# A hybrid decoder layer: the decode stream beside the prompt's input projection and attention

## What is computed

```python
def mixer_inputs(x, mod, w_in, cos, sin):
    z = modulate(x, mod[:, 0], mod[:, 1]) @ w_in            # 1024 -> 3072 columns
    h, gb, gc, q, k, v = jnp.split(z, SPLIT_IDX, axis=-1)   # 512 columns each
    q, k = apply_rope(q...), apply_rope(k...)
    return h, gb, gc, q, k, v

# prompt: causal differential attention over its own 1024 tokens, 4 heads, 2 components
y_conv = gb * short_conv(gc * h, conv_w)
s = q . k * QK_HEAD ** -0.5;  p = softmax(s);  a = p[:, :, 0] - lam * p[:, :, 1];  o = a @ v
# sample: the same, with k and v = gathered pages of cache_k, cache_v, then the new tokens
k_past = cache_k[l, page_table];  v_past = cache_v[l, page_table]
# both: output projection, adaLN gate, layer norm, SwiGLU of width 2816, gate, layer norm
```

## Time and profile before

| | us |
|---|---|
| median of 3 runs | 2172.3 (2167.52 to 2173.88) |
| the profiled execution, its own time | 2174.06 |
| span of its profile | 2172.3 |
| adaLN modulation | 0 to 97 |
| prompt turned and split | 97 to 120 |
| input projection, by feature | 122 to 262 |
| input projection, by token | 265 to 411 |
| sample's q, k, v; barrier; page numbers | 411 to 432 |
| decode stream, keys alone | 432 to 509 |
| decode stream beside the prompt's attention | 509 to 1056 |
| decode stream, values alone | 1056 to 1139 |
| output projection to the end | 1139 to 2172 |

### The profile page before, as it was taken

How to read it: one execution, slowest core, us unless ns; L and a number is a source line. 1 busy time by engine, 2 the same in 40 slices (tenths; PEclk the granted TensorE clock), 3 DMA queues, 4 the chain that set the end, 5 groups by cost and what they waited for, 6 DMA issues and landing times.

```text
span 2172.3 us, 39883 instructions
## 1 busy us (share of the span) xinstructions
PE 1791.4 (82%) x17492; PEld 1460.1 (67%) x17492; DVE 1049.0 (48%) x1596; ACT 542.2 (25%) x1151; POOL 321.1 (15%) x287
## 2 busy tenths in 40 slices
PE   4789999756777877777656957999999998999991
PEld 1267899644555555565546956777777776999991
DVE  2234221288788788888405573111112111566567
ACT  0210111003334234244212031112111110444441
POOL 0000000033333333333221026000000000000003
PEclk8799999858998889889857988999999999999996
DMA  9801123299999999999974100121121122611112
GB/s 301 310 20 40 57 78 116 81 406 397 411 387 408 413 408 404 406 392 415 340 272 175 58 20 20 59 96 58 58 77 58 58 64 88 226 45 45 45 35 99
DMA packets 133275, 404.29 MB, mean 186 GB/s; under 512 B 12153, under 2 KB 76665, under 8 KB 100338
## 3 DMA queue, kind: packets, MB, share of 16 engines
q0 software_dynamic: 37392, 270.55, 30.9%
q1 hardware_dynamic: 93666, 130.67, 17.8%
q10 hardware_dynamic: 2080, 1.05, 0.2%
HBM read 377.79 MB, written 24.51 MB: 185 GB/s over the span
## 4 chain that ended last, share of the span: by engine, by line
PE 65%; DMA 16%; DVE 14%; issue 3%; ACT 2%; POOL 0%; SPq 0%; DVEq 0%; ACTq 0%; POOLq 0%
PE psum L764 29%; PE psum L1051 12%; PE psum L772 11%; DMA v_ring<-cache_v,page_idx 10%; DVE k_ring L1489 4%; DMA ada_w<-w_ada 3%; PE psum L896 2%; PE psum L833 2%; PE psum L853 2%; PE psum L747 2%; DMA k_ring<-cache_k,page_idx 2%; DVE soft L1432 1%; DVE x_lo L1330 1%; PE psum L710 1%; DVE p_t L441 1%
## 5 line engine op out<-in xcount | busy, mean ns | idle before, releaser
L1489 DVE STREAM_TRANSPOSE k_ring<-k_ring 128x2048 f32<-128x2048 f32 x128 | 294.5, 2303 | 9.8 <-DMA k_ring<-cache_k,page_idx 9.5
L764 PE MATMUL psum<-x_hi,w_hi 128*128 128x512 f32 x896 | 281.3, 395 | 0.0
L764 PE MATMUL psum<-x_lo,w_hi 128*128 128x512 f32 x896 | 277.2, 391 | 0.0
L764 PE MATMUL psum<-x_hi,w_lo 128*128 128x512 f32 x896 | 275.9, 389 | 0.0
L1349 DVE TENSOR_TENSOR w_lo<-w_raw,w_hi 128x2048 fp32r<-128x2048 f32 x37 | 86.9, 2350 | 362.5 <-ACT w_hi L1109 352.6
L896 PE MATMUL psum<-v_ring,p_t 128*32 128x128 f32 x4096 | 161.3, 305 | 75.3 <-DMA v_ring<-cache_v,page_idx 73.5
L1051 PE MATMUL psum<-d_hi,h_hi 128*128 128x256 f32 x704 | 202.8, 288 | 13.1 <-DVE d_lo L1743 11.2
L1051 PE MATMUL psum<-d_lo,h_hi 128*128 128x256 f32 x704 | 200.2, 284 | 0.0
L1051 PE MATMUL psum<-d_hi,h_lo 128*128 128x256 f32 x704 | 200.0, 284 | 0.0
L764 PEld LDWEIGHTS psum<-x_hi,w_hi 128*128 128x128 f32 x896 | 165.6, 188 | 44.8 <-ACT h_out L1242 4.5
L764 PEld LDWEIGHTS psum<-x_lo,w_hi 128*128 128x128 f32 x896 | 168.7, 188 | 35.7
(11 more groups left out here) (228 smaller groups left out, 2610.5 us busy)
## 6 DMA issues: line engine op xcount, KB each, us to landing
ada_w<-w_ada SPq DMA_DIRECT2D x12, 2048.0 KB, 9.9
w_raw<-w_in SPq DMA_DIRECT2D x12, 1024.0 KB, 5.3
w_raw<-w_gate SPq DMA_DIRECT2D x11, 1024.0 KB, 5.4
w_raw<-w_up SPq DMA_DIRECT2D x11, 1024.0 KB, 6.2
h_store<-h_out SPq DMA_DIRECT2D x11, 1024.0 KB, 7.7
h_all<-h_store SPq DMA_DIRECT2D x11, 1024.0 KB, 8.9
d_raw<-w_down SPq DMA_DIRECT2D x44, 256.0 KB, 2.9
x_rows<-x_prompt SPq DMA_DIRECT2D x2, 2048.0 KB, 17.4
```

The costliest lines, as they stand in the source:

```text
L764: last = mm(psum[:, 2 * ft + c, 0:CH], w[:, s, k, ft * P:(ft + 1) * P], x[:, k, c * CH:(c + 1) * CH], start=k == 0 and j == 0, stop=k == K ...
L1489: v.transpose(group, group).then_inc(k_turned, 1)
```

## The change

Stages 2 and 3 become one. The sample tokens no longer share the prompt's weight blocks: their whole projection runs first, in 6 blocks of 512 columns loaded for them alone (`w_sample`, 2 MB each), one after each of the first 6 steps of the prompt's projection. So `w_in` is read twice. POOL's gathers start when these 6 products are done.

There are now 180 **turns** (`TURNS`), and `upto` gives the slots that lie in each:

- turns 0 to 23, half a **unit** of 128 convolution columns each (`half_unit`, 24 products of 512 tokens); a unit's weights are half a MB in pieces of 512 bytes, two buffers. Slots 0 to 21 lie in turns 10 to 23 (`FIRST`), 1 or 2 in a turn, keys alone.
- turns 24 to 71, one token tile of a 256-column block each (`tile_in`), 8 turns a block, blocks in the order q, k, v, q, k, v. Slots 22 to 69: two in the first turn of a block, none in the fifth, one in each other. `block_raw`, `block_hi`, `block_lo` and `z_rows` have one buffer each. Three PSUM banks (5 to 7) take the results of units and tiles, where there were four pairs.
- turns 72 and 73, two slots each. SP stores the last block, waits for it, and fetches head 0's keys and queries and all values of the prompt.
- turns 74 to 179, the prompt's attention as before, with 81 slots spread over 106 turns.

`k_ring` has 4 buffers instead of 5. The gates of the adaLN (`gate_p`, `gate_s`) give their room to the convolution: they are written to DRAM after stage 1 and fetched again ahead of `x1`, and `xs_rows` is fetched again too. What comes after the merged stage is as before.

```diff
-    GP, RK, RV = 4, 5, 3
+    GP, RK, RV = 4, 4, 3
+        FIRST = 10
+        upto = [0] * FIRST + [round((LAG - 2) * (p + 1 - FIRST) / (HALVES - FIRST)) for p in range(FIRST, HALVES)]
+        for p in range(TILES_IN):
+            upto.append(upto[-1] + {0: 2, 4: 0}.get(p % NT, 1))
+        upto += [upto[-1] + 2, upto[-1] + 4]
+        rest = SLOTS - upto[-1]
+        upto += [upto[-1] + rest * (p + 1) // (TURNS - HEAD0) for p in range(TURNS - HEAD0)]
...
-            pool.wait_ge(stage_done, 8)
-            pool.wait_ge(conv_s_in, 96)
-            pool.dma_start(v_rows[:], v_out.rearrange("(t p) n -> p t n", p=P)).then_inc(v_in_rows, 16)
+            pool.wait_ge(s_done, 2 * BLOCKS)
             pool.wait_ge(page_idx_ready, GP)
             load_pages(pool)
...
+            def keep_tile(n):
+                j, t = n // NT, n % NT
+                act.wait_ge(tm_done, n + 1)
+                if n == 0:
+                    act.wait_ge(y_conv_kept, 16 * (CC // P))
+                    act.wait_ge(conv_stored, 16 * (CC // P))
+                elif t == 0:
+                    act.wait_ge(z_stored, 16 * j)
+                copy(z_rows[:, t, :], psum[:, DENSE + n % 3, 0:WB]).then_inc(tm_free, 1)
...
+                for n in slots_at(p):
+                    slot(n)
+                if p < HALVES:
+                    half_unit(p)
+                    if p < BLOCKS:
+                        sample_in(p)
+                    if 1 <= p <= BLOCKS:
+                        fold_sample_in(p - 1)
+                    if p == BLOCKS + 2:
+                        turn_queries()
+                elif p < HALVES + TILES_IN:
+                    tile_in(p - HALVES)
...
             sp.wait_ge(o_turned, NT)
+            sp.dma_start(gate_p[:], gate_store[0:1].rearrange("o g d -> (o g) d").partition_broadcast(P)).then_inc(gates_in, 16)
+            sp.dma_start(gate_s[:], gate_store[1:1 + QUAD]).then_inc(gates_in, 16)
             sp.dma_start(x1[:], x_dram.rearrange("(t p) d -> p t d", p=P)).then_inc(x1_in, 16)
```

More of the change, by code:

```diff
@@ L531, in _ @@
-            for n in range(2, NB_IN):
-                load_w(n, w_in, in_cols[n])
-                if n == 6:
-                    sp.wait_ge(conv_ready, 1)
-                    with nc.allow_non_contiguous_dma(reason="two tokens' rows by feature"):
-                        for f in range(CC // P):
-                            sp.dma_start(io["new_conv_prompt"][0, 0][:, f * P:(f + 1) * P].rearrange("j p -> p j"),
-                                         u_conv[:, f, T:T + 2]).then_inc(conv_stored, 16)
-                if n - 2 >= 6:
-                    store_z(n - 8)
@@ new lines, in store_conv, with store_y @@
+            def store_conv(f):
+                sp.wait_ge(conv_ready, f + 1)
+                with nc.allow_non_contiguous_dma(reason="two tokens' rows by feature"):
+                    sp.dma_start(io["new_conv_prompt"][0, 0][:, f * P:(f + 1) * P].rearrange("j p -> p j"),
+                                 u_conv[:, T:T + 2]).then_inc(conv_stored, 16)
+            def store_y(f):
+                sp.wait_ge(fm_free, 6 * f + 6)
+                sp.dma_start(y_conv_store[f * P:(f + 1) * P, :], y_conv_f[:]).then_inc(y_conv_kept, 16)
@@ new lines, in store_z @@
+            def store_z(j):
+                half, which = j // 3, j % 3
+                if which < 2:
+                    sp.wait_ge(roped, 2 * half + which + 1)
+                else:
+                    sp.wait_ge(tm_free, TB + NT * (j + 1))
+                to = (q_store, k_out, v_out)[which]
+                sp.dma_start(to[:, half * WB:(half + 1) * WB].rearrange("(t p) n -> p t n", p=P), z_rows[:]).then_inc(z_stored, 16)
+            for p in range(HALVES):
+                if p % 2 == 0 and 2 + p // 2 < UNITS_IN:
+                    load_unit(2 + p // 2)
+                if p < BLOCKS - 2:
+                    load_sample(p + 2)
+                if p == 9:
+                    store_sample()
+                if p % 6 == 5:
+                    store_conv(p // 6)
+                if p > 6 and p % 6 == 1:
+                    store_y(p // 6 - 1)
@@ L555, in _ @@
             sp.wait_ge(conv_stored, 16 * (CC // P))
[L556 to L566 removed]
+            sp.wait_ge(y_conv_kept, 16 * (CC // P))
@@ new lines, in tile_in @@
+            def tile_in(n):
+                j, t = n // NT, n % NT
+                pe.wait_ge(w_lo_done, UNITS_IN + j + 1)
+                if n < 3:
+                    pe.wait_ge(fm_free, HALVES - 2 + n)
+                else:
+                    pe.wait_ge(tm_free, TB + n - 2)
+                at = slice(t * P, (t + 1) * P)
+                for k in range(KC):
+                    w_low = block_lo[k // (KC // 2)][:, k % (KC // 2), :]
+                    for i, (w, x) in enumerate(((block_hi[:, k, :], x_hi), (block_hi[:, k, :], x_lo), (w_low, x_hi))):
+                        last = mm(psum[:, DENSE + n % 3, 0:WB], x[:, k, at], w,
+                                  start=k == 0 and i == 0, stop=k == KC - 1 and i == 2)
+                last.then_inc(tm_done, 1)
@@ new lines, in sample_in @@
+            def sample_in(n):
+                if n == 0:
+                    pe.wait_ge(xs_ready, 1)
+                    pe.wait_ge(x_banks_free, 4 + UNITS)
+                pe.wait_ge(ada_in[n % 2], 16 * (z.MODS + n // 2 + 1))
+                pe.wait_ge(s_quads_free, 2 * n)
+                for k in range(KC):
+                    q = QUAD * (k % 4)
+                    last = mm(psum[q:q + QUAD, n % 2, :], x_t_in[:, k, :], w_sample[:, n % 2, k, :],
+                              start=k < 4, stop=k >= KC - 4)
+                last.then_inc(s_done, 2)
@@ new lines, in fold_sample_in, with turn_queries @@
+            def fold_sample_in(n):
+                pe.wait_ge(s_quads_free, 2 * n + 4)
+                if n >= 2:
+                    pe.wait_ge(s_fold_free, 2 * n)
+                mm(psum[0:QUAD, 2 + n % 2, :], C("quad_fold"), quads_in[:, n % 2, :], start=True, stop=True).then_inc(s_folded, 2)
+            def turn_queries():
+                pe.wait_ge(q_wide_ready, 1)
+                for hb in range(4 * H):
+                    last = mm(psum[:, 4, hb * BS:(hb + 1) * BS], q_wide[:, hb].rearrange("p a j -> p (a j)"),
+                              ident[0:QUAD, 0:QUAD], start=True, stop=True)
+                last.then_inc(q_all_done, 1)
@@ L955, in slot @@
                     by_query(b - 2)
-            for n in range(SLOTS):
-                h, u, q = dense_at(n)
+            for p in range(TURNS):
+                h, u, q = dense_at(p)
                 if u is None and q == 1:
@@ L1426, in maxima @@
+            ROPED = [j for j in range(BLOCKS) if j % 3 < 2]
             def maxima(u, c):
```

510 lines of the change are left out of this document (302 added, 208 removed).

## The result

The changed kernel takes 2178.1 us in the median (20 runs, 2171.2 to 2189.1) against 2169.4 for the kernel before (20 runs, 2159.8 to 2183.0). The ratio is 1.0045, 95% interval 1.003 to 1.006: slower by 0.45%. I had forecast 2160, so the sign was wrong; the time lies in the range.

The account below looks back on a forecast made before the run. PE was taken to bound the projection and full DMA engines the attention, whose turns were almost as slow by themselves. The merged stage's terms ended at 1124 against 1139; with 3 us after it, -12, so 2160 us, range 2100 to 2230.

Parts of the forecast that it names:

- so 547 - 41 - 45 = 461: Prompt's attention, turns 75 to 179: 547 us minus 41 of value waits and 45 of work moved or gone gives 461.
- the 22 for fifty transposes: Attention: fifty fewer key transposes, a third of them holding up a tile's chain by 1.3 us, save 22 us.
- rival B: Attention: the tile's chain, not its slots, sets 506 us; blocks wait 8 us; 2211 us in all; chance 0.20.
- The 15 for softmax moved ahead: Attention: a quarter of the sample's softmax pieces on DVE and ACT moved ahead, estimated to save 15 us.
- Turns 0 to 23: Units, sample projection and first key groups: 187 us from a start at 119, so turn 24 starts at 306.
- Turns 24 to 71: Projection tiles beside the stream: PE 262, block starts 21, waits for stores 32, sum 315 us; turn 72 at 621.
- The store term: Projection tiles: each block waits 0 to 9 us for the previous block's store, taken as 6.5 x 5 = 32.
- handoffs "at an estimated 0.15": Projection: handoffs between PE's pieces at 0.15 us each; 96 of them beside the tiles, 14 us.
- Turns 72 to 75: Before head 0's keys: last store, k and q queue behind about 11 outstanding gathers, 41 us, bounds 20 and 67.
- After it: After the merged stage: refetched gates delay x1 by 0 to 3 us; with xs_rows, 3 us taken.
- Rival A: Merged stage: transfers set the pace, stores land within PE's 19 us, head 0's fetches take 25; 2109 us; chance 0.20.
- Rival C: Projection tiles: coupled engine lists stall, a turn costs 8 us instead of 6.6, 384 instead of 315; 2229 us; chance 0.10.

## Why the prediction was wrong

**What bounds the attention.** I had read that "taking slots out of these turns helps only where a slot was on the tile's chain", and that most of the worth depends on this. That was the right question with the wrong answer in figures. The runs by the groups in the attention:

| run | groups | attention, us | waits for values | PE idle | clock |
|---|---|---|---|---|---|
| stream where it was, new code | 207 | 555 | 35 | 135 | 0.88 |
| no slots in the units' turns | 176 | 530 | 28 | 141 | 0.86 |
| the changed kernel | 132 | 489 | 0 | 147 | 0.85 |
| PE's groups alone | 132 | 433 | - | 120 | 0.87 |
| no stream | 0 | 488 | - | 242 | 0.57 |

(Groups are the records of the two lines divided by 32, PE idle is length less busy time.) From 207 to 132 groups the attention gains 66 us, but 35 of that are waits for values; the other 75 groups' work gives 31 (some us less if the 555 is too long, as said above), or 0.4 us a group, where PE alone takes 0.98 for one.

**The term that failed** is "so 547 - 41 - 45 = 461": 489 was measured, 28 more. The waits for values did go (43.0 us in the whole of 508 to 1055), and the 22 for fifty transposes is made likely by the 15 to 24 us that fifty others were worth. What I left out is that a value wait or a slot also covers the tile's chain. While PE waited for a value group, maximum, exponentials and combining went on; take the wait away and PE arrives earlier at the same chain. I counted these covers as pure gain. The chain waits grew by 62 us (34.8 + 26.5 for `a_rows` and `e_rows`, 0.5 for `a_t`). In the account of PE the attention became 58 us shorter: 77 us less busy, 43 us less waiting for values, and 62 us more waiting for the chain. Two runs bear it out: with nothing of the stream but PE's groups these waits are 115 of after's 125 us, and with 22 slots put back they fall to 92. A smaller part is the clock: it fell from 0.88 to 0.85, and the attention's own products grew from 184 to 193 us by their lines, of which some 2 us are records missing from the trace before. This is rival B, to which I gave 0.20, by the mark that I had set for it ("if PE's waits for `a_rows`, `a_t` and `e_rows` grow by 40 us or more, B"), at about six tenths of its price: it said 506, and the attention came out above the 473 that I had named as the point from which the change is slower.

The 15 for softmax moved ahead was an estimate whose share of the listed rows is not worked out, and the 8 for the last 35 turns has no row behind it; no run here measures them apart.

**Turns 0 to 23** ended as forecast: last unit product near 306, first key group at 199.5. Turn 24's two slots began at 305.9 for 306 forecast, but its first tile began at 317. In the run without a stream PE waited 10 us for block 0's lower halves there (277.6 to 287.6), and I had charged 2 (within the next stretch). In the changed kernel the lower halves were ready at 311.9. PE stood for 7.4 us in the second slot, before a transpose of the softmax, until DVE had copied the one before it to `p_t` (314.90 to 316.12), and this copy stood behind the lower halves and a key transpose in DVE's list. Error +9.

**Turns 24 to 71**: 315 forecast, 299 measured. The store term was 32, and the run with half stores shows 34. The rest I put at 283; counted from turn 24's slots, as the forecast did, it was 276 there (308.0 to 583.7). The handoffs "at an estimated 0.15" are the likeliest to have been too high: between the stalls a turn with one slot takes 4.95 us (602.64 to 607.59), where 2.9 + 2 x 0.98 + 2 x 0.15 gives 5.16, or 10 us more in 48 turns.

```profile
600.45 1.01 PE psum L989 x32
601.46 0.87 PE psum L1008 x32
602.33 0.31 PE psum L1021 x2
602.64 3.07 PE psum L889 x24
...
607.59 3.07 PE psum L889 x24
```

The store did not cost 6.5 us in each block but 10 to 11 us in every second one (PE stood before 385.9, 486.7 and 590.6), 32.7 in all: the total of 32 was met, by luck, with each stall mis-sized. **Turns 72 to 75**: 41 forecast, 34 measured; the reason given, the outstanding gathers, is shown by the fetches' 4.6 and 5.9 us once they are held back, and by the 10.5 us without a stream. **After it**: +3 forecast, +4.5 measured (the stage ends where it ended before, the span is 4.5 longer), with a fetch of `x` of 16.3 us in the chain. In the sum:

| | forecast | measured | difference |
|---|---|---|---|
| start, and turns 0 to 23 | 306 | 317 | +11 |
| turns 24 to 71 | 315 | 299 | -16 |
| turns 72 to 75 | 41 | 34 | -7 |
| attention | 461 | 489 | +28 |

That is +16, which leads from 1123 to 1139 and from a saving of 12 us to a loss of 4.5 in the profiled executions (8.7 in the medians). The first two rows are cut at the first tile; cut at turn 24's slots, as in the forecast, they are 0 and -5. Misses of -12 ahead of the attention covered nearly half of its +28: that is luck.

**Rival A** asked for stores that land in under 12 us; the quickest took 16.6, and four took over 26. With them the Trainium skill's figure ("DMA: Bandwidth & Descriptors", Specifications), that pieces from 512 bytes on reach line rate, does not carry over to a store that shares the engines: this one has pieces of 1 KB and moved at 1.05 MB / 26.4 us = 40 GB/s. **Rival C** fell as well: a turn of turns 24 to 71 cost 299 / 48 = 6.2 us, not 8.

**Where the expected gain went.** PE's idle time is where it was: 36 us of it lay beside the values alone and 35 beside the keys alone before; now 45 lie in turns 24 to 71, 33 of them behind the stores, 22 on the way to head 0's keys, and 20 more than before in the attention. The 33 us that the new form costs by itself are not to be added to this, since the slots cover most of its waits. With the stores in halves and the slots of the units' turns moved behind, the same idea is worth 2%.

## What to carry to other kernels

A wait on an in-order engine is also cover: before counting its removal as a gain, ask which chain ran on meanwhile, and take as a floor what the stage needs with the cover gone, measured by leaving the covered work out, with the clock in view. A store from a single buffer is to be priced by its landing time beside the transfers that will run next to it, not by its time alone, and half a buffer can hide it. When work is moved out of a stage that is bound by a chain, look at the clock of that stage as well.

## What the runs showed of the hardware

**TensorE's clock took back what an emptier stage saved.** Idle for half of the attention, PE was granted 0.57 and did the tile's products in 253 us by their lines; busy for 72% of it, it was granted 0.87 and did them in 184. Adding 139 us of products made the stage 56 us shorter.

**Transfers of small pieces slow down several times beside gathers.** 1 MB in pieces of 1 KB: 26.4 us (16.6 at the least) against 6.4; 0.5 MB in pieces of 512 bytes: 25.2 against 4.6. The gathers' pieces are 8 KB (1.05 MB over 128 partitions), and in turns 24 to 71 one of the values' landed in 10.7 us in the median. The Trainium skill ("DMA: Bandwidth & Descriptors", Queues, rings and completion order) says that each engine takes its queues in turn, a packet of some descriptors from each. If packets hold equally many pieces, a store of 1 KB pieces gets one ninth of 404 GB/s, so 1.05 MB takes an estimated 23 us, and a fetch of 512-byte pieces one seventeenth, 22 us for 0.52 MB. Both lie near what was measured; that this is the reason was not shown.
